# One matmul per head for the SSD exponents, and a re-ordered opening, in a four-sublayer diffusion backbone

## The reference

```python
sh1, sc1, g1, sh2, sc2, g2 = jnp.split(s_lat @ w_ada[i] + b_ada[i], 6, axis=-1)
a_lat = modulate(rmsnorm(x_lat, norm1_w[i]), sh1, sc1)        # h * (1 + scale) + shift
zxbcdt = h @ w_in                                             # z, x, B, C, dt
xbc = jax.nn.silu(dwconv_centred(xbc, conv_w, conv_b))        # 5 taps
dt = softplus(dt + dt_bias)
a_cum = jnp.cumsum(dt * a, axis=-1)                           # per head, in chunks of 128
wmat = cb[:, :, None] * _segsum_exp(a_cum)                    # exp(a_cum[l] - a_cum[s]), masked
y_diag = jnp.einsum('bghcls,bcsghp->bclghp', wmat, xd)
```

## Time and profile before

| | |
|---|---|
| median of 3 runs | 1379.88 us (1379.84 to 1380.93) |
| profiled execution, its own time | 1384.11 us |
| span of the profiled execution | 1382.4 us |
| granted TensorE clock, mean | 0.942 of full speed |
| PE busy | 1230.9 us, 89% |
| DVE / ACT / POOL busy | 925.8 (67%) / 581.8 (42%) / 113.5 us (8%) |
| first group's transposes (L1386) begin | 112.83 us |
| last group's scan ends (L1461) | about 488 us |

### The profile page before, as it was taken

How to read it: one execution, slowest core, us unless ns; L and a number is a source line. 1 busy time by engine, 2 the same in 40 slices (tenths; PEclk the granted TensorE clock), 3 DMA queues, 4 the chain that set the end, 5 groups by cost and what they waited for, 6 DMA issues and landing times.

```text
span 1382.4 us, 20652 instructions
## 1 busy us (share of the span) xinstructions
PE 1230.9 (89%) x7274; PEld 726.2 (53%) x7274; DVE 925.8 (67%) x1445; ACT 581.8 (42%) x1005; POOL 113.5 (8%) x127
## 2 busy tenths in 40 slices
PE   6779888898898879969999999997999977799997
PEld 6335454454454534424444444443765535688886
DVE  4984664674675678988788787664527756755654
ACT  2444553553653543233333332222334544566642
POOL 0003024015015100000000000000000000000000
PEclk9999999998998969979999999998999987899998
DMA  9213102202202034625555555431222101355553
GB/s 391 79 71 107 62 16 76 91 15 76 91 31 92 1 121 156 239 91 216 196 195 217 198 188 190 186 102 74 91 94 90 61 30 37 134 211 196 185 196 107
DMA packets 24957, 172.88 MB, mean 125 GB/s; under 512 B 2768, under 2 KB 2768, under 8 KB 6608
## 3 DMA queue, kind: packets, MB, share of 16 engines
q1 hardware_dynamic: 19008, 129.28, 25.7%
q0 software_dynamic: 5184, 37.75, 7.6%
q10 hardware_dynamic: 720, 5.24, 1.1%
HBM read 171.22 MB, written 1.05 MB: 125 GB/s over the span
## 4 chain that ended last, share of the span: by engine, by line
PE 63%; DVE 20%; ACT 7%; issue 5%; DMA 1%; POOL 1%; DVEq 1%; ACTq 0%; SPq 0%; POOLq 0%
PE bank L1295 17%; PE bank L1297 17%; PE bank L1296 17%; DVE arena L871 4%; ACT arena L447 2%; ACT wh L390 2%; DMA x<-xT 1%; PE bank L1585 1%; DVE arena L756 1%; DVE arena L803 1%; PE bank L1410 1%; PE bank L1599 1%; DVE arena L798 1%; DVE arena L933 1%; DVE hl L794 1%
## 5 line engine op out<-in xcount | busy, mean ns | idle before, releaser
L1295 PE MATMUL bank<-hh,wh 128*128 128x512 f16 (+1 forms) x1152 | 403.3, 350 | 35.4 <-DVE hl L794 15.8
L726 DVE SCALAR_TENSOR_TENSOR wl<-raw,wh 128x1024 f16<-128x1024 f32 (+1 forms) x232 | 267.9, 1172 | 234.3 <-ACT wh L390 232.3
L1296 PE MATMUL bank<-hl,wh 128*128 128x512 f16 (+1 forms) x1152 | 403.4, 350 | 0.0
L1297 PE MATMUL bank<-hh,wl 128*128 128x512 f16 (+1 forms) x1152 | 402.9, 350 | 0.0
L390 ACT ACTIVATE wh<-raw 128x1024 f16<-128x1024 f32 (+1 forms) x232 | 229.9, 1011 | 284.8 <-PE bank L1297 214.5
L1295 PEld LDWEIGHTS bank<-hh,wh 128*128 128x128 f16 x1152 | 114.7, 100 | 148.7 <-issue 64.6
L1295 PE MATMUL bank<-arena,wh 128*128 128x512 f16 (+1 forms) x544 | 181.6, 334 | 10.2 <-DVE wl L726 3.1
L1296 PE MATMUL bank<-arena,wh 128*128 128x512 f16 (+1 forms) x544 | 181.4, 333 | 0.0
L1297 PE MATMUL bank<-arena,wl 128*128 128x512 f16 (+1 forms) x544 | 181.4, 333 | 0.0
L756 DVE SCALAR_TENSOR_TENSOR arena<-arena,araw 128x1024 bf16<-128x1024 f32 x144 | 167.6, 1219 | 0.2
L1297 PEld LDWEIGHTS bank<-hh,wl 128*128 128x128 f16 x1152 | 115.2, 100 | 98.0 <-issue 10.6
(11 more groups left out here) (194 smaller groups left out, 1395.1 us busy)
## 6 DMA issues: line engine op xcount, KB each, us to landing
raw<-wgu SPq DMA_DIRECT2D x44, 1024.0 KB, 4.8
arena<-wadaT POOLq DMA_DIRECT2D x36, 1024.0 KB, 5.0
raw<-wdn SPq DMA_DIRECT2D x16, 896.0 KB, 4.6
raw<-wxg SPq DMA_DIRECT2D x8, 1024.0 KB, 4.9
raw<-wz SPq DMA_DIRECT2D x8, 1024.0 KB, 4.8
raw<-wout SPq DMA_DIRECT2D x8, 1024.0 KB, 4.8
raw<-wdn SPq DMA_DIRECT2D x8, 1024.0 KB, 4.9
raw<-wqk SPq DMA_DIRECT2D x8, 1024.0 KB, 4.8
```

The source lines that it names most:

```text
L726: ve.scalar_tensor_tensor(wl[:, u.slot, a:b], raw[:, u.slot, a:b], WS, wh[:, u.slot, a:b], ALU.mult, ALU.subtract).then_inc(lo_done, 1)
L1295: pe.matmul(o, wh[:, u.slot, wsl], ahi[:, k, t0:t1], start=st, stop=False)
L1296: pe.matmul(o, wh[:, u.slot, wsl], alo[:, k, t0:t1], start=False, stop=False)
L1297: i = pe.matmul(o, wl[:, u.slot, wsl], ahi[:, k, t0:t1], start=False, stop=en)
```

## The change

1. **Exponents from rows.** The prefix sums of dt*a are computed once, for all heads, as rows (head on the partition, token in the free dimension) by 48 short matmuls after `A_mm`, split in three bfloat16 parts that lie in partitions 0 to 31, 32 to 63 and 64 to 95 of `AT`. In the scan one matmul per head, with a selecting column `pick` as the stationary operand and 96 partitions, takes the place of the two. One small DVE copy (`ATg`) takes the place of two per group (`adgh`, `adgl`).
2. **A new opening.** SP loads constants and `x` right after the columns. All eight first adaLN units are done on PE with the condition vector stationary (32 columns wide, the rest zero) and the weights moving (256 columns), in four column tiles of the array, each taking two of the eight 128-row blocks; ACT copies the partial sums out and PE adds and turns them (`ada0_turn`). The DVE part (`aturned`, `afdump`, the first `crow`) goes. `x` times the inverse root goes into a buffer `nx` ahead of time; scale, shift and splitting are shared by ACT (even tiles) and DVE (odd tiles).
3. **B, C and dt in one pass.** B and C are one unit; PE does, tile by tile of the input, B, C and dt, so it can start with the first tile. There are three units in the opening in place of four, and `U_GRP` is 3. The order of casts, conversions and convolutions on ACT and DVE is changed to fit.

```diff
-U_GRP = 4
+U_GRP = 3
@@ sync
-            load_first(0)
-            sp.dma_start(araw[:, :], crow).then_inc(crow_in, 16)
-            load_turned(0)
...
-            load_group(Unit(U_SSD0), 0)
+            sp.dma_start(kp[:, :], keep).then_inc(in_kp, 16)
+            sp.dma_start(x[:, :, :], xT).then_inc(in_x, 16)
+            for n in range(6):
+                load_first(n)
+            load(Unit(U_SSD0), wxg[0, :, 0:2048])
+            sp.dma_start(dtraw, wdt).then_inc(in_dt, 16)
+            load_first(6)
+            load_first(7)
+            load(Unit(U_SSD0 + 1), wxg[0, :, 2048:4096])
+            sp.dma_start(stg, stage).then_inc(in_stage, 16)
+            load(Unit(U_SSD0 + 2), wxg[0, :, 4096:6144])
@@ scalar
+            def hi0(k):
+                if k % 2 == 0:
+                    for b, a, e in [(0, 0, TC), (1, TC, T)]:
+                        i = act.activation(nx[:, k, a:e], nx[:, k, a:e], ACT.Identity, scale=wsc[:, k, b:b + 1], bias=wsh[:, k, b:b + 1])
...
+                act.activation(hh[:, k, :], nx[:, k, :], ACT.Copy).then_inc(hh_ok, 1)
...
+            u = Unit(U_SSD0)
             act.wait_ge(pads_ok, 2)
-            evac_pre(Unit(U_SSD0), 0, 0, 0)
+            evac_pre(u, 0, 0, 0)
+            evac_pre(u, 0, 1, 1)
+            cvt(u.plus(2))
...
             silu_xbc(0, 0)
-            evac_pre(u.plus(1), 0, 1, 1)
-            cvt(u.plus(3))
             ldt = PR[:, LDT].rearrange("p c h -> p (c h)")
             act.wait_ge(adt_ok, 1)
             act.activation(ldt, ldt, ACT.Ln).then_inc(ln_ok, 1)
-            cvt(u.plus(4))
+            evac_pre(u.plus(1), 0, 2, 2)
             silu_xbc(0, 1)
-            evac_pre(u.plus(2), 0, 2, 2)
-            evac_pre(u.plus(2), 0, 3, 3)
+            evac_pre(u.plus(1), 0, 3, 3)
+            cvt(u.plus(3))
             silu_xbc(0, 2)
             silu_xbc(0, 3)
+            act.wait_ge(at_mm, 1)
+            for d in range(2):
+                act.activation(AT[0:AROWS, d, :], (YB, AB)[d][0:AROWS, :], ACT.Copy).then_inc(at_hi, 1)
             act.wait_ge(A_mm, 1)
...
             act.activation(dst, dst, ACT.Exp).then_inc(aexp, 1)
+            for d in range(2):
+                act.wait_ge(at_rest, d + 1)
+                act.activation(atm[0:AROWS, d, :], atr[0:AROWS, d, :], ACT.Copy).then_inc(at_mid, 1)
+                act.activation(AT[32:64, d, :], atr[32:64, d, :], ACT.Copy).then_inc(at_mid, 1)
             for m in range(2):
-                evac_pre(u.plus(3), 0, 4 + m, m)
+                evac_pre(u.plus(2), 0, 4 + m, m)
                 silu_xbc(0, 4 + m)
@@ vector
             conv_tile(0, 0)
+            cvt(Unit(U_SSD0 + 2))
             ve.wait_ge(dta, 2)
...
+            conv_tile(0, 1)
             cvt(u.plus(3))
-            conv_tile(0, 1)
-            cvt(u.plus(4))
             conv_tile(0, 2)
             conv_tile(0, 3)
...
+            for d in range(2):
+                ve.wait_ge(at_hi, d + 1)
+                ve.tensor_tensor(atr[0:AROWS, d, :], (YB, AB)[d][0:AROWS, :], AT[0:AROWS, d, :], ALU.subtract).then_inc(at_rest, 1)
             conv_tile(0, 4)
+            for d in range(2):
+                ve.wait_ge(at_mid, 2 * d + 2)
+                ve.tensor_tensor(AT[64:AROWS, d, :], atr[64:AROWS, d, :], atm[64:AROWS, d, :], ALU.subtract).then_inc(at_ok, 1)
             conv_tile(0, 5)
@@ tensor
+            def ada0(a):
+                pe.wait_ge(in_ada[a], 16)
+                if a >= 4:
+                    pe.wait_ge(a0_out, a - 3)
+                for n in range(2):
+                    for q in range(4):
+                        k = 4 * n + q
+                        i = pe.matmul(GB[a % 4][32 * q:32 * q + 32, 0:UN], s2w[:, k, :], afirst[:, a, k * UN:(k + 1) * UN],
+                                      start=(n == 0), stop=(n == 1))
+                i.then_inc(a0_part, 1)
...
+            for d in range(2):
+                for g in range(NG):
+                    for n, half in enumerate((adh, adl)):
+                        at_ = (d * NG + g) * 32
+                        for part in range(3):
+                            o = (YB, AB)[d][32 * part:32 * part + 32, g * P:(g + 1) * P]
+                            i = pe.matmul(o, half[:, at_:at_ + 32], masks[:, d, :], start=(n == 0), stop=(n == 1))
...
                     for h in range(4):
-                        hc = (2 * c + d) * HG + 4 * hq + h
-                        for m, half in enumerate((adgh, adgl)):
-                            i = pe.matmul(o[:, h * P:(h + 1) * P], half[:, hc:hc + 1].to_broadcast([P, P]), masks[:, d, :],
-                                          start=False, stop=(m == 1), skip_group_check=True)
+                        row = c * HG + 4 * hq + h
+                        i = pe.matmul(o[:, h * P:(h + 1) * P], pick[0:AROWS, row:row + 1].to_broadcast([AROWS, P]), ATg[0:AROWS, d, :],
+                                      start=False, stop=True, skip_group_check=True)
```

More of the change, by code:

```diff
@@ L1341, in _ @@
-            i.then_inc(a0_mm, 1)
-            bcast(0, 0)
+                    i = pe.matmul(AB[:, o:o + 2], apart4[:, a, m * P:(m + 1) * P], sum4, start=True, stop=True)
+                if a == ADA_FIRST - 1:
+                    i.then_inc(a0_mm, 1)
+            pe.wait_ge(s2_ok, 2)
+            ada0(0)
+            ada0(1)
+            pe.wait_ge(in_kp, 16)
+            pe.wait_ge(ssd, KC)
+            ssum(0, 0)
+            ada0_turn(0)
+            ada0(2)
+            bcast(0, 0)
+            for a in range(3, ADA_FIRST):
+                ada0_turn(a - 2)
+                ada0(a)
@@ L1345, in _ @@
+            ada0_turn(ADA_FIRST - 2)
+            ada0_turn(ADA_FIRST - 1)
             u = Unit(U_SSD0)
-            gemm(u, [(0, GB[0][:, :])], H, range(KC), 0, KC - 1, width=P, ready=(h_ok, 0))
+            pe.wait_ge(lo_done, u.half + (LO + 2))
             pe.wait_ge(dtl_ok, 1)
             pe.wait_ge(c_rt, 1)
-            for c in range(NCH):
-                tk = slice(c * P, (c + 1) * P)
-                for k in range(KC):
+            for k in range(KC):
+                pe.wait_ge(h_ok, k + 1)
+                for m in range(2):
+                    wsl = slice(m * D + k * P, m * D + (k + 1) * P)
+                    pe.matmul(GB[m][:, :], wh[:, u.slot, wsl], hh[:, k, :], start=(k == 0), stop=False)
+                    pe.matmul(GB[m][:, :], wh[:, u.slot, wsl], hl[:, k, :], start=False, stop=False)
+                    i = pe.matmul(GB[m][:, :], wl[:, u.slot, wsl], hh[:, k, :], start=False, stop=(k == KC - 1))
+                if k == KC - 1:
+                    i.then_inc(unit_done, 2)
+                for c in range(NCH):
+                    tk = slice(c * P, (c + 1) * P)
@@ L1356, in _ @@
+                    i = pe.matmul(o, hh[:, k, tk], dtl[:, w_], start=False, stop=(k == KC - 1), skip_group_check=True)
             i.then_inc(dt_mm, 1)
-            gemm(u.plus(1), [(0, GB[1][:, :])], H, range(KC), 0, KC - 1, width=P)
-            gemm(u.plus(2), [(0, GB[2][:, :]), (1, GB[3][:, :])], H, range(KC), 0, KC - 1)
-            pe.wait_ge(masks_ok, 4)
+            gemm(u.plus(1), [(0, GB[2][:, :]), (1, GB[3][:, :])], H, range(KC), 0, KC - 1)
+            pe.wait_ge(masks_ok, 7)
             pe.wait_ge(adt_ok, 1)
@@ L1366, in _ @@
-            for n, half in enumerate((adh, adl)):
-                i = pe.matmul(OB[1][:, 256:512], masks[:, 2, :], half, start=(n == 0), stop=(n == 1))
-            i.then_inc(A_mm, 1)
+                    pe.matmul(o, mask, by_group(half)[:, :, a4], start=(n == 0), stop=(n == 1))
+            for j in range(2):
+                a4 = slice(NG * j, NG * j + NG)
+                o = OB[1][:, 256:512].rearrange("p (c a h) -> p c a h", c=NCH, a=2 * NG)[:, :, a4]
+                for n, half in enumerate((adh, adl)):
+                    i = pe.matmul(o, masks[:, 2, :], by_group(half)[:, :, a4], start=(n == 0), stop=(n == 1))
@@ L1369, in _ @@
+            i.then_inc(A_mm, 1)
+            for d in range(2):
+                for g in range(NG):
+                    for n, half in enumerate((adh, adl)):
+                        at_ = (d * NG + g) * 32
+                        for part in range(3):
+                            o = (YB, AB)[d][32 * part:32 * part + 32, g * P:(g + 1) * P]
+                            i = pe.matmul(o, half[:, at_:at_ + 32], masks[:, d, :], start=(n == 0), stop=(n == 1))
+            i.then_inc(at_mm, 1)
             pe.wait_ge(pre_ok, 2)
-            gemm(u.plus(3), [(0, GB[0][:, :]), (1, GB[1][:, :])], H, range(KC), 0, KC - 1)
+            gemm(u.plus(2), [(0, GB[0][:, :]), (1, GB[1][:, :])], H, range(KC), 0, KC - 1)
```

191 lines of the change are left out of this document (95 added, 96 removed).

## The result

The changed kernel takes 1384.41 us (median of 11 runs, 1377.86 to 1386.14), the kernel before 1379.84 us (median of 11 runs, 1377.21 to 1383.59). The ratio is 1.0032, with a 95% interval of 1.0018 to 1.0046: 0.3% slower, where 0.5% faster was forecast. The ratios leave out runs more than 1.5% above the fastest of their kernel; there was one such run, of e3, at 1405.29 us. The profiled execution of the changed kernel took 1385.78 us, with a span of 1384.1 us.

What follows compares the result with a forecast made beforehand. No engine alone bounds the groups; the opening waits for the adaLN scales, later for DVE. Groups -5.5, opening -2.7 and first group's clock +1.4 make -6.8 us: median 1373.1 from 1379.9, with 8 of 10 cases in 1362 to 1380.

Steps and rivals of the forecast that it cites:

- Part 2: Opening's load order: `x` lands at 12.0 us, the first adaLN unit at 14.5, then one each 2.5 us.
- Part 3: Opening's adaLN on PE: 1.0 to 2 us per unit, scales ready at 39.3 us, 4.8 earlier than 44.1.
- Parts 4 and 5: Opening from scales to groups: dt at 57.8 us, `adt_ok` at 73.8, sixth convolution ends at 107.0, 2.7 us earlier.
- The charge of 1.4 us: First group: PE waits 3 us for the transposes, and the lower clock after it lengthens the group by 1.4 us.
- Part 1: Exponent blocks in the groups: halved matmuls save 4.6 us of the chain, plus 0.9 toward the last group's end, 5.5 together.
- Rival (c): Groups: longer PE waits drop its clock, three drops of 3.4 us each, giving 1383 us; chance 0.12.

Runs made afterwards that it cites:

- e3: The changed kernel with idle matmuls (6, 2, 2, 2) in the four chunks of the last group: median 1384.26 us, ratio 1.0006 to the kernel before.
- e6: The changed kernel with the row casts moved later, under the last two convolutions: 1380.90 us, ratio 1.0003 to the kernel before.
- e2: The changed kernel with the old exponents put back, so new opening only and no row casts: 1375.30 us, ratio 0.9957 to the kernel before.
- e1: The kernel before with only the exponents from rows and their casts, old opening kept: 1384.63 us, ratio 1.0032 to the kernel before.
- e5: The changed kernel with each exponent matmul followed by one that adds zeros, eight matmuls a block again: 1382.43 us, ratio 1.0014 to the kernel before.
- e9: The changed kernel with both the casts moved later and the zero-adding matmuls: 1376.29 us, ratio 0.9974 to the kernel before.
- e11: The changed kernel unaltered, timed and profiled once more: 1384.96 us, ratio 1.0038 to the kernel before.
- e4: The changed kernel with 12 idle matmuls in PE's wait before each group's first transposes: 1376.18 us, ratio 0.9964 to the kernel before.
- e7: New opening with old exponents, plus 12 idle matmuls before each group's first transposes: 1374.21 us, ratio 0.9957 to the kernel before.
- e8: The kernel before with 12 idle matmuls before each group's first transposes: 1380.05 us, ratio 0.9990 to the kernel before.

## Why the prediction was wrong

**Part 2 (loads)** held: `x` at 12.16 for 12.0 us, the first adaLN unit at 14.73 for 14.5.

**Part 3 (adaLN on PE)** was right in the unit, 1.93 us for "1.0 to 2", and wrong in the order. PE works in order: the root's sum (L1348) waited for nothing but took the place of unit 3, and the broadcast (L1354) at 23.50 that of unit 4, so units that had landed began at 21.64 and 26.15. After that no time could be caught up, because each unit is followed by its turning matmuls, which the prediction had only behind the last unit: 2.81 us from 26.15 to 28.96, more than one load's 2.5. The scales came at 42.7, not 39.3. The prediction gave the root's branch a price on DVE and ACT and none on PE. Its 6.8 us for serial work is also a little low by its own row: from L1400 to the next matmul it is 0.89 us (107.76 to 108.65), so 2048 columns at half clock are 7.1.

**Parts 4 and 5** held, shifted by these 3.4 us. Scales to dt: 18.6 us for 18.5. dt to `adt_ok`: 15.8 for 16.0. `adt_ok` to the sixth convolution's end: 33.4 for 33.2, of which the casts are 4.0 (e6, which has them elsewhere, and e2, which has none, both take 29.3), and 3.7 forecast. The opening therefore ended 0.8 us later than before in this execution, not 2.7 earlier.

**The charge of 1.4 us** for the first group did not come: it took 102.1 us for 104.5. That it and the 3.4 us of Part 3 work against each other is, as far as the profiles tell, why the opening alone came out so near (5.9 us for 5.0), which is luck. Neither is firm to better than 2 us: the first copies of one and the same kernel lay 2.4 us apart in two executions.

**Part 1 is the step that failed:** "half is 4.6 us", and 0.9 for the last group, sum 5.5. The block's time was right, as PE's timeline of the changed kernel has it (start to start 0.23 us for 0.22):

```profile
449.32 0.39 PE L1504 MATMUL bank<-arena 96*128 96x128 bf16 x4
449.55 0.38 PE L1500 MATMUL bank<-negm,idb 128*128 128x512 bf16 x1
```

Its size was about right as well, for the full groups at an equal clock: 1.2 to 1.5 us each, where 4.6 over three had been forecast. The step itself says that the other blocks' time lengthens PE's waits, 8.7 of the 14.2 us by its sum (11.9 in e1's profile). What the sum puts at nothing is what these longer waits do to the clock of the second and third group and of the last; the 1.4 us it charges are for the first. 2.33 us became 3.07 in the full groups, and in most of them the low time rose to 20.3 us or more, which takes 1.2 us back each. 1.72 us became 1.94 in the last group, and there the clock had fallen before the head products in three of five executions and stayed low for 10.2 us, where behind the shorter wait it was low for 3.4 us at most: 63.7 us for the 58.3 of e5, so +5.4 where -0.9 stood (+3.3 against the 60.4 of the profile before, whose last group began with 6.3 us at the low level; the change's began with 6.7, e5's with 3.4). Against e2's profile the change's three full groups come out even (313.4 for 313.2 us: 10.4 us more low time, and the gain at equal clock) and the last group is 6.4 us longer (63.7 for 57.3). The long low stretch was absent with the waits as before (e5, e9), with idle matmuls in the last group (e3, 59.8 us in the profile), and in e11's execution of the same kernel (58.7 us); e1's kept its clock with the longer wait too. So the longer wait goes with the low stretch in three of five executions and not always. That it is the cause is argued from these rows and from what the zeros and the idle matmuls of e4 win back.

**Rival (c)** had the mechanism and, by luck, the time, 1383. It looked at the wrong place: it expected the 1.25 us wait to pass 2 us, with 3.4 us for each of three drops, and the median came out at 1384.41. The waits behind which the clock changed were those that were already 2.3 and 1.7 us long. The longer low time of a full group cost 1.2 us, the drop in the last group about 5. That ACT and DVE set the pace behind the waits of the full groups would explain the small price, but no run shows it. It was given 0.12 because its "against" weighed only the 1.25 us wait. The earlier trace rows had the warning: at 152 to 156 us the clock stood at 0.85 behind a wait of this kind.

The account in ratios: opening -5.9; casts +4.0 (e6); the rest of the rows +6.3 where -5.5 was forecast; total +4.4. Of the 6.3, the zeros take back 2.5 alone and 4.0 with the casts moved (e6 to e9), and 2.3 stay open. Each of these differences is good to some 2 or 3 us either way. On the old opening the same rows cost 4.4 in all; e1's profiled execution shows no drop in the last group (58.5 us) and was 1.5 us under the median of its runs, so it does not show how often one comes there. Why one execution has the drop and another of the same kernel does not is open as well. Not tried were idle matmuls in the 3.07 us waits of the full groups' chunks themselves, for which there is no free bank.

## What to carry to other kernels

Work taken from an engine that alternates with others and does not bind alone can come back as waits (11.9 of 14.2 us between two profiles here); sum that engine's waits before and after, and don't price it by its share of the chain. On PE such a wait can cost its clock: list the waits that a saving will lengthen, the longest first. Small differences between two kernels need ratios of many runs: one kernel's profiled executions here differed by 7.3 us, and a stretch that no edit touches by 4. What a new computation adds on another engine (here six casts and two pairs of remainders) goes behind the work on which the chain waits, and an in-order engine needs its slow side branches placed where nothing ready stands behind them.

## What the runs showed of the hardware

The same kernel took 1384.1 and 1376.8 us of span in two executions, with the granted clock of one stretch at 0.50 and 1.00. The Trainium skill, "TensorE: Matmul & The Clock Gate", Part 1, says of a kernel's start that the count of slow matmuls changes from run to run with the gate's phase. The two executions agree that it changes from run to run, and show it 450 us into a kernel; whether by the phase, no run here shows.

Four float32 column tiles of 32 columns overlap almost fully. Eight matmuls of 256 columns took 1.93 us at the low level (read from L1354's 2.08 us), where the prediction's estimates were 6.8 for serial work and 1.7 for full overlap: 3.5 times. The Trainium skill, "TensorE: Matmul & The Clock Gate", Part 3, has three column tiles at 2.38 times; no run here has three.

A matmul that adds zeros, or computes nothing that is used, can shorten a kernel: 2.5 us by 256 of one kind (4.0 with the casts moved), 9.4 us by 48 of the other. On the kernels with eight matmuls a block, the 48 gave nothing that can be measured (e7, e8).
